# Ring slots of down rows: five of eight summed by TensorE and three by VectorE, instead of four and four

## What is computed

```python
def peer_ffn(h, wq, subkeys, u, v):      # per token: 8 heads x 16 experts = 128 experts
    q = (h @ wq).reshape(B, S, 8, 2, 128)
    sub_scores = einsum('bshpk,hpnk->bshpn', q, subkeys)
    top_v, top_i = top_k(sub_scores, 16)
    cand = top_v[..., 0, :, None] + top_v[..., 1, None, :]
    best_v, best_pos = top_k(cand, 16)                 # -> expert (B,S,128), gates = softmax
    ub = take(u, expert)                               # "up rows", 128 of 1024 floats per token
    hid = gelu(einsum('tkd,td->tk', ub, x)) * gates
    vb = take(v, expert)                               # "down rows"
    return einsum('tk,tkd->td', hid, vb)
```

## Time and profile before

| | us |
|---|---|
| median of 3 runs (lowest, highest) | 3070.01 (3066.22, 3072.72) |
| the profiled execution's own time | 3074.66 |
| its span, first to last instruction | 3072.9 |
| gathers, first issue to last issue (POOL L474) | 1470.2 to 3053.1 |
| down rows, block 0, first issue to the next phase's | 1680.3 to 1876.9 |
| down rows, block 1 | 2118.2 to 2312.1 |
| down rows, block 2 | 2493.4 to 2688.5 |
| down rows, block 3, to the end of the span | 2871.0 to 3072.9 |
| busy: PE, DVE, POOL, ACT | 1985.6, 1828.9, 1237.3, 510.2 |

### The profile page before, as it was taken

How to read it: one execution, slowest core, us unless ns; L and a number is a source line. 1 busy time by engine, 2 the same in 40 slices (tenths; PEclk the granted TensorE clock), 3 DMA queues, 4 the chain that set the end, 5 groups by cost and what they waited for, 6 DMA issues and landing times.

```text
span 3072.9 us, 26861 instructions
## 1 busy us (share of the span) xinstructions
PE 1985.6 (65%) x9164; PEld 1412.9 (46%) x9164; DVE 1828.9 (60%) x3552; ACT 510.2 (17%) x1213; POOL 1237.3 (40%) x1156
## 2 busy tenths in 40 slices
PE   7869989989999899849620773246661036700376
PEld 6756678878998878637420221245220012200122
DVE  5662331345344423662999778854779877698644
ACT  3012333242011123312000111001110001100011
POOL 4230000420000113170446666643666666666665
PEclk9965569999999998559855997568996569955789
DMA  6630003212222212002679999965999999999998
GB/s 231 250 117 1 14 28 124 89 56 84 88 97 85 94 68 104 1 28 83 255 260 391 352 331 348 382 256 198 346 351 361 366 368 342 351 362 372 364 363 302
DMA packets 170792, 665.47 MB, mean 217 GB/s; under 512 B 19616, under 2 KB 20144, under 8 KB 160176
## 3 DMA queue, kind: packets, MB, share of 16 engines
q0 software_dynamic: 147456, 536.94, 46.6%
q1 hardware_dynamic: 23216, 127.00, 11.3%
HBM read 661.76 MB, written 2.10 MB: 216 GB/s over the span
## 4 chain that ended last, share of the span: by engine, by line
PE 40%; POOL 18%; DVE 16%; issue 13%; DMA 6%; another core or an unknown queue 4%; ACT 1%; SPq 0%; DVEq 0%; POOLq 0%; ACTq 0%
POOL weights L474 17%; PE bank L798 7%; PE bank L799 7%; PE bank L800 7%; PE bank L1136 4%; DVE weights L1497 3%; PE bank L889 3%; DMA weights<-in_peer_v,scratch 3%; DVE bank L1524 3%; PE bank L836 2%; PE bank L872 2%; PE bank L850 1%; PE bank L856 1%; DMA scratch<-in_w_ada 1%
## 5 line engine op out<-in xcount | busy, mean ns | idle before, releaser
L1090 PE MATMUL bank<-weights,gain_row 128*128 128x512 f32 x1024 | 529.0, 646 | 397.3 <-issue 211.5
L474 POOL DMA_INDIRECT weights<-in_peer_u,scratch x512 | 485.6, 949 | 421.5 <-issue 139.0
L1497 DVE CUSTOM_DVE_ANT_0 weights<-weights,bank 128x1024 f32<-128x1024 f32 x512 | 609.8, 1220 | 48.9 <-issue 20.2
L474 POOL DMA_INDIRECT weights<-in_peer_v,scratch x512 | 492.4, 962 | 262.7 <-issue 159.3
L1090 PEld LDWEIGHTS bank<-weights,gain_row 128*128 128x128 f32 x1024 | 186.4, 200 | 736.1 <-issue 569.9
L395 POOL CAST weights_split<-weights 128x2048 fp32r<-128x2048 f32 x25 | 51.0, 2041 | 998.9 <-DMA weights<-in_w_in 543.7
L1524 DVE SCALAR_TENSOR_TENSOR bank<-weights,scratch,bank 128x1024 f32<-128x1024 f32 x252 | 324.7, 1289 | 204.1 <-DMA weights<-in_peer_v,scratch 152.4
L1136 PE MATMUL bank<-h_T,area 128*128 128x128 f32 x1024 | 147.8, 300 | 119.0 <-issue 118.8
L1078 PE MATMUL bank<-ident,h_T 128*128 128x128 f32 x32 | 6.9, 386 | 322.7 <-DVE scratch L1514 301.8
L798 PE MATMUL bank<-h_T_high,weights_split 128*128 128x512 f32 (+1 forms) x528 | 208.5, 395 | 7.9 <-POOL weights_split L396 7.9
L799 PE MATMUL bank<-h_T_low,weights_split 128*128 128x512 f32 (+1 forms) x528 | 207.4, 393 | 0.0
(11 more groups left out here) (260 smaller groups left out, 3547.3 us busy)
## 6 DMA issues: line engine op xcount, KB each, us to landing
weights<-in_w_ff SPq DMA_DIRECT2D x32, 1024.0 KB, 4.8
scratch<-in_w_ada SPq DMA_DIRECT2D x48, 512.0 KB, 5.7
weights<-in_w_in SPq DMA_DIRECT2D x22, 1024.0 KB, 5.2
area<-in_w_pq SPq DMA_DIRECT2D x4, 2048.0 KB, 10.6
weights<-in_peer_u,scratch POOLq DMA_INDIRECT x512
weights<-in_peer_v,scratch POOLq DMA_INDIRECT x512
weights<-in_w_out SPq DMA_DIRECT2D x4, 1024.0 KB, 5.8
weights<-in_w_mk SPq DMA_DIRECT2D x4, 1024.0 KB, 4.8
```

The costliest lines, as they stand in the source:

```text
L474: pool.indirect_dma_start(ring[k], None, src, index).then_inc(row_landed[k], 16)
L1090: ins = pe.matmul(bank[half][:], wdiag[:, i, :], ring[k][:, half * COLS:(half + 1) * COLS], start=(first and i == 0), stop=(last and i == ...
L1497: dve.tensor_tensor_reduce(out=ring[k], in0=ring[k], in1=pair[2][:], scale=1.0, scalar=0.0, op0=ALU.mult, op1=ALU.add, accum_out=hid[:, r: ...
```

## The change

`SHARED` names five slots instead of four. Everything else follows from it: `wdiag` gets a fifth buffer, ACT builds five diagonals a turn, PE sums five rows a turn (ten matmuls), DVE three. DVE keeps slots 0, 3 and 6, PE has 1, 2, 4, 5 and 7. Which slot is first and which is DVE's last is the same as before.

```diff
-SHARED = range(1, RING, 2)
+SHARED = (1, 2, 4, 5, 7)
```

## The result

| | before | after |
|---|---|---|
| median of 5 runs, us | 3066.22 | 3085.3 |
| lowest, highest | 3060.76, 3072.72 | 3082.24, 3086.17 |
| profiled execution, own time | 3074.66 | 3085.72 |
| its span | 3072.9 | 3084.0 |
| down phases of blocks 0, 1, 2 | 196.6, 193.9, 195.1 | 204.7, 195.7, 198.4 |

The ratio is 1.0058, with a 95% interval of 1.0041 to 1.0075. The forecast was 3062, its range 3052 to 3074: wrong in sign. The two profiled executions lie only 11 us apart and the medians 19, because the profiled one of before was 8 us above its median.

A forecast was written before the change was run, and what follows sets the result against it. Down phases were taken as bound by transfer, with DVE holding the ring at slot 0. Profiled 3074.66 - 9.9 (DVE) + 0.9 (PE holding) + 0.25 (end) = 3065.9, median 3061.3, stated as 3062 us; range 3052 to 3074.

The forecast's parts named there:

- the stops: DVE idle in step 2 with no releaser in the core, 4.08 us in block 1; might land elsewhere with shorter code.

The follow-up runs named there:

- b1: The kernel before with two extra, already satisfied waits on DVE in each turn of blocks 0 to 2; 2886.68 us, ratio 0.9997.
- e0: The changed kernel itself, unaltered, measured again in another set against the kernel before; 2885.66 us, ratio 0.9995.

## What to carry to other kernels

Idle time that the trace puts down to nothing in the core is a term of the sum like any other: list where it falls now, how much of it lies in slack, and price its moving in both directions before trusting a gain of a few us. Before taking work from an engine that holds a ring, ask whether the stretch between its last row of a turn and its next first row grows. With slots 0, 3 and 6 it does not; with 0, 2 and 4 it does, and POOL lost 30.6 us at slot 0 instead of 61.2. Even so that kernel was only level with the kernel before (1.000). Repeat a comparison of half a per cent in another set before carrying it over: the same two kernels measured 1.0058 in one and 0.9995 in another.

## What the runs showed of the hardware beyond what I expected

- The same program takes 2887 or 3066 us, by the set and not by the chip alone; the whole difference arises in the gather phases (first gather at about 1470 us in both). Some 70 us of it lie in block 1's up phase alone (241 us before, 171 in b1), where POOL waits once for 60.7 us in the kernel before: DVE waits there 58.2 us in `prepare` for the queries of PE and ACT, and within that phase PE stood idle for 184 us in 115 gaps ahead of the queries' matmuls (L1136), against 48 us in 4 gaps in e0. DVE is busy for 1828.9 us in the one and 1825.6 in the other (b1), POOL for 1237.3 and 1243.4.
- Where the stops are absent, POOL issues block 3's 128 down gathers in 163 us, 1.28 each, and 408 GB/s pass; where they are present, 182.
- One extra 512 KB copy from HBM to HBM for every eight gathers costs 4% (f1).
- ACT and POOL are held together for 3 to 6 us while PE goes on, every 22 to 28 us in block 3 of the kernel before; in the blocks with pick steps DVE often is too (at 1861 us all three go on within 0.3 us).
